# Hybrid decoder step: token numbers of the first expert pass from rank products on TensorE, router products on unscaled rows, and the samples' state product placed between the memory heads

## The chip, the core and the metric

The kernel runs on one core of one Trainium2 chip. The metric is the device time of one launch in microseconds (us), as the median of several runs. The core's engines run their own instruction streams side by side and wait for each other through semaphores: PE (TensorE, matrix products and transposes), DVE (VectorE), ACT (ScalarE), POOL (GpSimd, which here also issues the indirect DMAs), and SP (SyncE, which here only issues DMAs, so it is called the load queue).

## The reference, cut to what matters

One layer of a decoder trunk handles 512 prompt tokens and 8 sample tokens (520 rows of width 1024). A mixer with two head groups (a matrix memory of four heads, and windowed attention of eight heads) is followed by a mixture of 32 experts of which each token takes four:

```
z  = rms_norm(x, norm1) @ w_in                    # one projection for both groups
m  = matrix memory of 4 heads over z              # samples: from a given state C (8,4,64,128)
a  = window attention of 8 heads over z           # samples: over a cache of 128 keys
y  = x + concat(m, a) @ w_out
xn = rms_norm(y, norm2)
logits = xn @ w_router + b_router                 # (520, 32)
top 4 of 32, gates = softmax of the four
for every expert: rows that chose it -> w_gate, w_up, w_down (all 1024 x 1024), times gate
y  = y + sum over the four experts;  out = rms_norm(y, final_norm)
```

For the samples the memory's result needs q @ C, q.k and q.n for each of the 32 pairs of sample and head, and a new state C' = decay C + k v. Those are what "the samples' state product" and "the state update" mean below.

## The kernel before

The work runs in four stages, and each engine's order is the order in which its program is written.

1. **Projection, attention and memory heads** (to about 230 us of the span). The memory heads go in 12 turns (`UNIT_TURN`); a unit is a head h and a block of 128 keys, 16 units in all. In each turn DVE multiplies a unit's weights by PE's scores (`products_of_turn`, L1250), makes the next unit's weights (`weights_of_turn`, L1241), and after a head's last unit closes the head (`finish_head`, L1263 to L1283). The four turns before the last eight ride on projection steps; the last eight (4 to 11) each begin with a filler on PE, one part of the output projection over the attention half (`out_part`). PE's value products of head 3 wait until `finish_head(2)` has emptied PSUM (`num_used`).
2. **From the heads to the first output rows.** ACT and DVE normalise the heads' rows, PE transposes them, DVE multiplies them by the output gate (`mixm_made`, L1322, after the sigmoid, `og_ready`). The samples' gates take an exponential, a logarithm and three more exponentials on ACT (L903 to L909), with four small DVE operations between (L1310 to L1316). The samples' state, 1 MB, is loaded into the buffer that held the heads' rows, so the load (L525) waits for the heads' transposes; then DVE multiplies it by the samples' queries and adds up (L1344 to L1352, the result is `part`), and PE sums `part` across partitions (`dsum`). PE's order is: `project(0)`, the replication of gates and values (`rep`), `dsum`, a few small sample products (`own`), `project(1)`. `project(i)` finishes the output projection of 128 rows. POOL adds the residual (L649): the prompt rows of tile 0 are loaded again (L527) once the stores of the prompt's final state have landed.
3. **Routing.** For each of four tiles of 128 rows and one tile of 8 samples: DVE adds the halves (`add_up`), ACT takes squares and a square root (`squares`), DVE scales the row by it and by norm2 (`scale_rows`, L1374), PE transposes the scaled row and ACT copies it (`evac_x2`), PE makes the logits with `w_rt` (`route`), DVE finds the top four (`choose`, which also ends with the gates and the combined gate table g3), PE counts how many earlier rows chose each expert (`ranks`), and DVE turns expert and rank into a place in a table (`places`, L1381 to L1386). The sample tokens' attention is woven between the tiles, and `mixs_ready` (the samples' mixed rows) releases the samples' output projection, `project(4)`. When `project(4)` is over, the load queue may begin with the expert weights: 1 MB pieces, 12 for an expert, in a ring of 8.
4. **Experts.** POOL writes each chosen (token, gate) pair to its place in a table in DRAM: 20 indirect DMAs, four a tile (L663, first after `mixs_ready`). When all 20 have landed it reads the table back (L668), copies the token numbers out of it (`pass_tok`, L681), gathers the rows of the first two experts (L676), and stores the starting sums of the output to DRAM (`acc_rows`, L690), which has to have landed before an expert's output is added (`added`). Meanwhile PE, ACT and DVE make the experts' output biases for all rows (L1540) and split the first three weight pieces into a rounded part and a rest (L1026 on ACT, L438 on DVE). Then a loop runs over the 32 experts: 12 pieces each, every piece split by ACT and DVE and multiplied by PE with 12 products of 128 x 96 by 512 columns (L1618).

## Time and profile before

| | |
|---|---|
| median of 3 runs | 1583.27 us (1581.88 to 1585.08) |
| the profiled execution | 1581.5 us, span 1579.8 us |
| busy share of the span | PE 93%, DVE 80%, ACT 67%, POOL 12% |
| mean granted clock of PE | 0.952 of full speed |
| the expert loop on PE (L1618, 128 x 96 by 512) | 4608 products, 1100.0 us |
| DMA | 464.78 MB, mean 294 GB/s |

The span is what the profiler covers of one launch. Busy shares are averages over stages with different limits: three quarters of the span is the expert loop, and the change touches only what stands between the projections and the loop's start, about 200 to 410 us.

### The profile page before, as it was taken

The page shows a single profiled execution, that of the slowest core. Times are in us where ns is not written, and L with a number is a line of the kernel's source. Part 1 is how long each engine was busy: PE and PEld are TensorE (multiplying, and loading weights), DVE is VectorE, ACT ScalarE, POOL GpSimd, SP SyncE. Part 2 cuts the span into 40 slices and gives each one's busy share as a digit, 9 for nine tenths or more (in the row PEclk, how much of TensorE's full clock was granted, in tenths as well). Part 3 has the DMA queues.
Part 4 walks back from the last instruction along what each step waited for, and adds up shares of the span by engine and source line. Part 5 has one row for each costly group of instructions (what it writes and reads, how often), then busy time and mean ns, then how long its engine had stood idle before and what let it go on. Part 6 is the DMA issues. An engine that isn't in the chain of part 4 may idle for free.

```text
span 1579.8 us, 21342 instructions
## 1 busy us (share of the span) xinstructions
PE 1462.6 (93%) x7155; PEld 1069.2 (68%) x7155; DVE 1264.5 (80%) x1175; ACT 1057.3 (67%) x961; POOL 183.2 (12%) x183
## 2 busy tenths in 40 slices
PE   6999985774999999999999999999999999999993
PEld 5999764652676767676676767676766767676762
DVE  4344357335798999999999999999999998999995
ACT  4455333332678777777777777777777777777874
POOL 3000012026001110000000011000000001100000
PEclk9999996765899999999999999999999999999997
DMA  7311315016899999999999999999999999999994
GB/s 220 115 54 55 87 46 139 31 32 237 302 369 368 367 355 371 365 378 369 374 367 369 369 361 370 357 375 370 381 364 370 369 366 366 363 369 360 383 353 152
DMA packets 170588, 464.78 MB, mean 294 GB/s; under 512 B 14220, under 2 KB 28184, under 8 KB 170280
## 3 DMA queue, kind: packets, MB, share of 16 engines
q1 hardware_dynamic: 157528, 432.03, 74.2%
q0 software_dynamic: 8880, 24.00, 6.5%
q10 hardware_dynamic: 4144, 8.31, 1.6%
q8 instruction: 18, 0.29, 0.1%
q14 instruction: 18, 0.15, 0.0%
HBM read 447.90 MB, written 23.59 MB: 298 GB/s over the span
## 4 chain that ended last, share of the span: by engine, by line
PE 65%; issue 13%; DVE 11%; ACT 5%; DVEq 2%; DMA 1%; ACTq 1%; POOL 1%; POOLq 0%; SPq 0%
PE ps L1618 62%; DVE ring_r L438 6%; PE ps L1621 3%; ACT ring_r L1026 2%; DVEq L1587 1%; ACT reg_a L1039 1%; DVE reg_b L1581 1%; DVE reg_b L1576 1%; DMA acc_rows<-reg_z 0%; DMA reg_b<-in_state_C 0%; DMA acc_rows<-reg_a,pass_tok 0%; ACT L726 0%; POOLq L683 0%; ACT ring L1087 0%; ACT reg_z L934 0%
## 5 line engine op out<-in xcount | busy, mean ns | idle before, releaser
L1618 PE MATMUL ps<-ring_r,reg_z_r 128*96 128x512 f32 x4608 | 1100.0, 395 | 7.7 <-DVE reg_z_r L1546 7.6
L1618 PEld LDWEIGHTS ps<-ring_r,reg_z_r 128*96 128x96 f32 x4608 | 737.4, 162 | 322.6 <-DVE ring_r L438 11.0
L438 DVE TENSOR_TENSOR ring_r<-ring,ring_r 128x2048 fp32r<-128x2048 f32 x387 | 868.1, 2283 | 81.7 <-ACT ring_r L1026 81.7
L1026 ACT ACTIVATE ring_r<-ring 128x2048 fp32r<-128x2048 f32 x387 | 735.8, 1915 | 166.7 <-PE ps L1618 165.7
L705 POOL DMA_INDIRECT acc_rows<-reg_a,pass_tok x32 | 46.1, 1441 | 1030.6 <-issue 994.3
L1618 PE MATMUL ps<-reg_a_r,ring_r 128*128 128x264 f32 (+1 forms) x576 | 110.1, 286 | 0.0
L1045 ACT ACTIVATE reg_z_r<-ps 128x384 fp32r<-128x384 f32 x130 | 59.0, 480 | 66.9 <-PE ps L1621 66.9
L1618 PE MATMUL ps<-ring_r 128*128 128x256 f32 (+3 forms) x372 | 103.7, 328 | 0.0
L1618 PEld LDWEIGHTS ps<-reg_a_r,ring_r 128*128 128x128 f32 x576 | 90.6, 188 | 2.4 <-issue 2.2
L676 POOL DMA_INDIRECT reg_a<-xhat_rows,pass_tok x34 | 71.6, 2106 | 20.8 <-issue 20.8
L1618 PEld LDWEIGHTS ps<-ring_r 128*128 128x128 f32 (+1 forms) x372 | 67.5, 183 | 8.8 <-issue 3.5
L1546 DVE TENSOR_TENSOR reg_z_r<-ps,reg_z_r 128x384 fp32r<-128x384 f32 x130 | 65.7, 546 | 9.5 <-ACT reg_z_r L1045 9.5
L1039 ACT ACTIVATE reg_a<-ps,reg_t 96x512 f32<-96x512 f32 x66 | 41.6, 679 | 15.5 <-PE ps L1618 15.3
L1588 DVE SCALAR_TENSOR_TENSOR reg_x<-reg_x,reg_b 96x512 f32<-96x512 f32 x64 | 44.1, 689 | 4.8
L863 ACT ACTIVATE reg_z<-ps 128x256 f32<-128x256 f32 (+1 forms) x36 | 13.8, 384 | 45.6 <-PE ps L1618 45.6
L1064 ACT ACTIVATE reg_b<-reg_b 96x1024 f32<-96x1024 f32 x32 | 34.0, 1064 | 14.2 <-DVE reg_b L1576 14.0
L1586 DVE TENSOR_SCALAR reg_x<-ps 96x512 f32<-96x512 f32 x64 | 43.4, 678 | 0.0
L1621 PE MATMUL ps<-ident,reg_a 96*128 96x96 f32 x264 | 27.9, 249 | 15.0 <-DMA reg_a<-xhat_rows,pass_tok 15.0
L1186 DVE SCALAR_TENSOR_TENSOR reg_w<-ps,reg_b 128x512 f32<-128x512 f32 (+1 forms) x16 | 10.0, 625 | 39.4 <-PE ps L1618 39.4
L1576 DVE TENSOR_SCALAR reg_b<-ps 96x512 f32<-96x512 f32 x64 | 40.9, 678 | 0.0
L1621 PEld LDWEIGHTS ps<-ident,reg_a 96*128 96x128 f32 x264 | 26.1, 143 | 21.0 <-issue 15.9
L1130 DVE TENSOR_TENSOR ring_r<-ring,ring_r 128x2048 fp32r<-128x2048 f32 x13 | 29.8, 2289 | 13.1 <-ACT ring_r L759 13.1
(302 smaller groups left out, 942.6 us busy)
## 6 DMA issues: line engine op xcount, KB each, us to landing
ring<-in_w_gate SPq DMA_DIRECT2D x131, 1024.0 KB, 7.3
ring<-in_w_up SPq DMA_DIRECT2D x128, 1024.0 KB, 5.3
ring<-in_w_down SPq DMA_DIRECT2D x128, 1024.0 KB, 8.5
ring<-in_w_in SPq DMA_DIRECT2D x9, 1024.0 KB, 6.6
ring<-in_w_out SPq DMA_DIRECT2D x4, 1024.0 KB, 5.2
ring<-in_x_prompt SPq DMA_DIRECT2D x4, 512.0 KB, 8.6
reg_x<-in_x_prompt SPq DMA_DIRECT2D x4, 512.0 KB, 7.0
xhat_rows<-reg_w ACTq DMA_DIRECT2D x4, 512.0 KB, 3.7
```

Of the source, the lines that this page charges most:

```text
L438: return eng.tensor_tensor(rest_r(k), w, rounded_r(k).bitcast(F32), ALU.subtract)
L676: pool.indirect_dma_start(xg[0:CAP, u, :], None, xhat_rows[:, :], bass.IndirectOffsetOnAxis(pass_tok[0:CAP, e:e + 1], 0), bounds_check=TT ...
L705: pool.indirect_dma_start(acc_rows[:, :], bass.IndirectOffsetOnAxis(pass_tok[0:CAP, e:e + 1], 0), yrow[0:CAP, u, :], None, bounds_check=AC ...
L1026: act.activation(rounded_r(k), ring[:, slot_of(k), :], ACT.Copy).then_inc(hi_ready, 1)
L1039: last = act.activation(yrow[0:CAP, u, 512 * q:512 * q + 512], ps[4 + q][0:CAP, :], ACT.Copy, scale=slot_tab[:, bass.ds(t2 + 1, 1)])
L1045: last = act.activation(out[:, 0, 4 * q:4 * q + 4, :], ps[bank + q][:, 0:4 * CAP].rearrange("p (c n) -> p c n", c=4), ACT.Copy)
L1546: last = dve.tensor_tensor(out[:, 1, 4 * q:4 * q + 4, :], ps[bank + q][:, 0:4 * CAP].rearrange("p (c n) -> p c n", c=4), out[:, 0, 4 * q:4 ...
L1576: last = dve.tensor_scalar(eG[0:CAP, 512 * q:512 * q + 512], ps[q][0:CAP, :], LIMIT, None, ALU.min)
L1586: dve.tensor_scalar(hrow[0:CAP, cs], ps[2 + q][0:CAP, :], LIMIT, -LIMIT, ALU.min, ALU.max)
L1588: dve.scalar_tensor_tensor(hrow[0:CAP, cs], hrow[0:CAP, cs], 1.0, eS[0:CAP, cs], ALU.add, ALU.mult).then_inc(h_ready, 1)
L1618: return pe.matmul(out, lhsT, rhs, start=start, stop=stop, skip_group_check=True)
L1621: return pe.transpose(out, in_, ident[0:k, 0:k])
```

## The change

**The samples' state product.** The state gets a buffer of its own (`c_state` in the ring's scratch, `c_prod` and `c_half` in the buffer of the heads' rows), so its load no longer waits for the heads' transposes: it is issued with the other sample inputs. POOL makes the sample masks after unit 6 and not after unit 15. DVE multiplies and adds up one half of the state after turn 7 and the other after turn 8, and does the gates' small operations after turns 7 and 9; ACT does their exponentials and logarithm in turns 8 and 10. After the heads, ACT takes the sigmoid first; PE makes `rep` before the heads' transposes and `dsum` before `project(0)`. The state update moves from behind `add_up(0)` to ahead of it.

**The router on unscaled rows.** norm2 is multiplied into `w_rt` once; `route` transposes the rows of y1 and no longer those of xhat; the logits are multiplied by the row's factor in `choose`. `scale_rows` and the gates (`gates_of`) move behind `choose` and `places`.

**Token numbers from rank products.** For each tile `places` also makes, for each of the four choices, a one-hot of the rank over 96 places (`at_rank`) and the token number in the chosen expert's column (`at_expert`); PE multiplies them (`slots_of`, four products of 96 x 32), and DVE adds the tiles up into `pass_tok`. POOL gathers the first two experts' rows as soon as `pass_tok` is there, and then makes the last four table entries, reads the table back (it still holds the gates) and stores the starting sums.

```diff
-            dve.wait_ge(dec_in, 16 * (DEC_IN - 1))
-            dve.wait_ge(masks_made, 1)
-            dve.scalar_tensor_tensor(d32[:, 0:1], gpre[:, 1:2], -1.0, gpre[:, 1:2], ALU.mult, ALU.max).then_inc(sample_dve, 1)
+                if turn == 7:
+                    dve.wait_ge(dec_in, 16 * DEC_IN)
+                    dve.wait_ge(masks_made, 1)
+                    dve.scalar_tensor_tensor(d32[:, 0:1], gpre[:, 1:2], -1.0, gpre[:, 1:2], ALU.mult,
+                                             ALU.max).then_inc(sample_dve, 1)
+                    query_states(0, part_half)
+                if turn == 8:
+                    query_states(1, part[:, 0:DV])
...
-            dve.tensor_tensor(p_v, c_v, q16.unsqueeze(2).to_broadcast([P, 16, DV]), ALU.mult)
...
-            dve.tensor_reduce(part[:, 0:DV], c_prod.rearrange("p (k v) -> p v k", k=16), AX_X, ALU.add)
...
+            dve.wait_ge(late_in, 64)
+            dve.tensor_tensor(w_rt, w_rt, cols[:, 8:16].unsqueeze(2).to_broadcast([P, KC, NE]), ALU.mult)
...
+                dve.scalar_tensor_tensor(id4[0:r, :], rank4[0:r, :], -1.0, own_id[0:r, i:i + 1].to_broadcast([r, TOPK]),
+                                         ALU.mult, ALU.add)
+                dve.tensor_tensor(at_rank[0:r], iota_r[0:r].unsqueeze(1).to_broadcast([r, TOPK, CAP]),
+                                  rank4[0:r, :].unsqueeze(2).to_broadcast([r, TOPK, CAP]), ALU.is_equal)
+                dve.drain()
+                dve.tensor_tensor(at_expert[0:r], rt_oh[i % 2][0:r].rearrange("p e k -> p k e"),
+                                  id4[0:r, :].unsqueeze(2).to_broadcast([r, TOPK, NE]), ALU.mult).then_inc(sel_ready, 1)
...
-                pe.wait_ge(xhat_ready, i + 1)
+                pe.wait_ge(y_ready, 2 * i + 2)
...
-                        last = tr(ps[4 + q][:, c * P:c * P + r], xhat[0:r, i % 2, (4 * q + c) * P:(4 * q + c + 1) * P], r)
+                        last = tr(ps[4 + q][:, c * P:c * P + r], y1[0:r, i, (4 * q + c) * P:(4 * q + c + 1) * P], r)
...
+            def slots_of(i):
+                r = rows(i)
+                pe.wait_ge(sel_ready, ROUTE_ORDER.index(("p", i)) + 1)
+                for k in range(TOPK):
+                    last = mm(ps[7][0:CAP, P:P + NE], at_rank[0:r, k, :], at_expert[0:r, k, :],
+                              start=(k == 0), stop=(k == TOPK - 1))
+                last.then_inc(rank_psum, 1)
...
+            pool.wait_ge(count_ready, 1)
+            gather(0, 0)
+            gather(1, 1)
+            scatter_entries(NT)
```

On DVE, in turns 6 to 8 of the heads, before: the rest of a weight piece (L1130), products and weights of units 11 to 13.

```order
L1130 TENSOR_TENSOR ring_r_61<-ring,ring_r_61 128x2048
L1250 TENSOR_TENSOR reg_t<-reg_t,ps 128x256
L1241 TENSOR_SCALAR reg_t<-reg_w,small 128x128
L1130 TENSOR_TENSOR ring_r_61<-ring,ring_r_61 128x2048
L1250 TENSOR_TENSOR reg_t<-reg_t,ps 128x128
L1241 TENSOR_SCALAR reg_w<-reg_w,small 128x512
L1241 TENSOR_SCALAR reg_w<-reg_w,small 128x384
L1250 TENSOR_TENSOR reg_w<-reg_w,ps 128x512
L1250 TENSOR_TENSOR reg_w<-reg_w,ps 128x384
```

And after the change, over the same turns (`reg_b` is now the half product, `reg_w` and `reg_c` the sums of the halves):

```order
L1153 TENSOR_TENSOR ring_r_63<-ring,ring_r_63 128x2048
L1332 SCALAR_TENSOR_TENSOR ring<-ring 32x1
L1312 TENSOR_TENSOR reg_b<-ring 128x1024
L1315 TENSOR_REDUCE reg_w<-reg_b 128x128
L1273 TENSOR_TENSOR reg_t<-reg_t,ps 128x128
L1264 TENSOR_SCALAR reg_w<-reg_w,small 128x512
L1264 TENSOR_SCALAR reg_w<-reg_w,small 128x384
L1312 TENSOR_TENSOR reg_b<-ring 128x1024
L1315 TENSOR_REDUCE reg_c<-reg_b 128x128
L1337 TENSOR_TENSOR ring<-ring 128x16
L1339 TENSOR_TENSOR reg_c<-reg_c,reg_w 128x128
```

The two halves of the state (the 128x1024 products and the 128x128 sums) now stand among the units' products; the rows L1344 to L1352 of before, behind the heads, are gone.

On POOL, from the pads of the tables to the starting sums, before:

```order
L657 ISA
L663 DMA slot_rows<-reg_t,entry_at 21504x2 x20
L668 DMA reg_t<-slot_rows 96x7x64
L672 TENSOR_LOAD count_i
L672 ISA x2
L681 COPY pass_tok<-reg_t 96x34
L676 DMA reg_a<-xhat_rows,pass_tok 96x1024 x2
L690 DMA acc_rows<-reg_z 128x1024 x4
L690 DMA acc_rows<-reg_z 8x1024
L691 DMA acc_rows<-reg_z 96x1024
```

And after:

```order
L672 ISA
L677 DMA slot_rows<-reg_t,entry_at 21504x2 x16
L689 DMA reg_a<-xhat_rows,pass_tok 96x1024 x2
L677 DMA slot_rows<-reg_t,entry_at 21504x2 x4
L704 DMA reg_t<-slot_rows 96x7x64
L706 TENSOR_LOAD count_i
L706 ISA x2
L709 DMA acc_rows<-reg_z 128x1024 x4
L709 DMA acc_rows<-reg_z 8x1024
L710 DMA acc_rows<-reg_z 96x1024
```

The two gathers have moved from behind the read-back of the table to ahead of the last four entries, and the starting sums follow the read-back.

On PE, from the heads' transposes to `project(1)`, before:

```order
L1621 MATMUL ps<-ident,reg_b 128x128 x16
L1618 MATMUL ps<-ring_r_61,reg_a_r_62 128x512 x24
L1618 MATMUL ps<-ring 128x130
L1618 MATMUL ps<-reg_t,ring 32x130
L1618 MATMUL ps<-ring 64x130
L1618 MATMUL ps<-ring 64x128
L1621 MATMUL ps<-ident,ring 128x64
L1618 MATMUL ps<-ring_r_61,reg_a_r_62 128x512 x24
```

And after:

```order
L1684 MATMUL ps<-ring 128x130
L1687 MATMUL ps<-ident,reg_b 128x128 x16
L1684 MATMUL ps<-reg_c,ring 32x130
L1684 MATMUL ps<-ring_r_63,reg_a_r_64 128x512 x24
L1684 MATMUL ps<-ring 64x130
L1684 MATMUL ps<-ring 64x128
L1687 MATMUL ps<-ident,ring 128x64
L1684 MATMUL ps<-ring_r_63,reg_a_r_64 128x512 x24
```

`rep` (128x130) and `dsum` (32x130) have moved ahead of `project(0)` (the first 24 products).

## Rows read from the trace of the kernel before

**Rows 1.** Busy by stretch: length, PE, PEld, DVE, ACT, POOL, clock, DMA, GB/s

```profile
230.00:262.00 32.00, 13.81 (x46) 10.43 (x47) 23.19 (x37) 12.22 (x17) 11.12 (x14) 0.65 0.60 157
262.00:357.00 95.00, 71.18 (x293) 54.57 (x291) 40.68 (x132) 31.38 (x52) 12.57 (x11) 0.69 0.14 44
357.00:397.00 40.00, 14.60 (x67) 10.34 (x67) 19.58 (x39) 11.72 (x16) 23.57 (x23) 0.52 0.71 255
```

**Rows 2.** Waits of the load queue, 500 to 1500: total, times, longest

```profile
SPq L113 <- PE ps L1618: 788.5, 334, 3.5
```

**Rows 3.** Chain that ended last: start, us, what; heads to project(1)

```profile
237.40 1.28 ACT L903
...
244.13 6.30 DMA reg_b<-in_state_C
250.45 2.29 DVE ring L1344
...
255.11 3.65 DVE reg_t L1347
...
263.08 7.43 PE ps L1618 x24
```

**Rows 4.** Waits by engine, 240 to 480: total, times, longest

```profile
PE ps L1618 <- ACT reg_z L934: 11.8, 5, 4.1
...
PE ps L1621 <- DVE reg_w L1374: 7.5, 2, 5.0
...
PE ps L1618 <- DVE entry_at L1386: 2.5, 1, 2.5
```

**Rows 5.** Timeline of PE: start, us, what, count, idle before

```profile
222.84 1.83 PE L1618 MATMUL ps<-reg_t,reg_w 128*128 128x129 f32 x14
...
246.98 8.58 PE L1618 MATMUL ps<-ring_r,reg_a_r 128*128 128x512 f32 x24 [2.89 <-issue]
...
356.66 0.16 PE L1621 MATMUL ps<-ident 1*1 1x1 f32 x1
...
397.10 1.17 PE L1618 MATMUL ps<-reg_t_r,reg_p_r 128*96 128x512 f32 x2 [2.08 <-DVE reg_z_r L1546]
```

**Rows 6.** Timeline of DVE, same columns

```profile
219.73 0.76 DVE L1273 TENSOR_TENSOR reg_b<-ps,gsc 128x256 f32<-128x256 f32 x2
...
252.66 2.38 DVE L1345 TENSOR_TENSOR ring<-ring 128x16 f32<-128x16 f32 x1
...
373.57 6.27 DVE L1540 TENSOR_TENSOR reg_z<-reg_z,ps 128x512 f32<-128x512 f32 x10 [2.63 <-PE ps L1618]
...
379.89 6.68 DVE L438 TENSOR_TENSOR ring_r<-ring,ring_r 128x2048 fp32r<-128x2048 f32 x3
```

**Rows 7.** Timeline of POOL, same columns

```profile
251.83 5.50 POOL L649 TENSOR_TENSOR reg_z<-reg_z,reg_x 128x1024 f32<-128x1024 f32 x2 [19.27 <-DMA reg_x<-in_x_prompt]
...
345.79 1.12 POOL L663 DMA_INDIRECT slot_rows<-reg_t,entry_at  x1 [1.02 <-issue]
...
368.10 0.98 POOL L663 DMA_INDIRECT slot_rows<-reg_t,entry_at  x1 [0.30 <-issue]
```

**Rows 8.** Timeline of the load queue: the reload of prompt tile 0

```profile
244.75 0.33 SPq L527 DMA_DIRECT2D reg_x<-in_x_prompt  x1
```

**Rows 9.** Chain that ended last, from project(4) to the expert loop

```profile
364.22 0.18 DVE reg_t L1392
...
366.04 2.35 PE ps L1618 x10
...
374.71 4.46 issue
...
382.38 4.26 POOLq L683
...
389.29 1.04 POOL reg_a L676
...
394.34 7.66 DMA acc_rows<-reg_z
```

More of the change, by code:

```diff
@@ L253, in hybrid_step @@
         q16, k16, n16, kw16 = d_in[:, 0:16], d_in[:, 16:32], d_in[:, 32:48], d_in[:, 48:64]
-        part = reg_t[:, 0:132]
+        part = reg_c[:, 2048:2048 + 132]
+        part_half = reg_w[:, 1540:1540 + DV]
         part2 = part[:, 0:130]
@@ L657, in _, with scatter_entries @@
             pool.engine_nop().then_inc(pads_made, 1)
-            pool.wait_ge(tab_init, 16)
-            for i in range(NTILE):
+            def scatter_entries(i):
                 pool.wait_ge(entries_ready, i + 1)
@@ L666, in _ @@
                         bounds_check=PASSES * CAP * NE - 1, oob_is_err=False).then_inc(entries_out, 16)
-            pool.wait_ge(entries_out, ENTRIES)
-            pool.dma_start(slot_tab[:, 2:2 + (PASSES + 1) * TABW].rearrange("p (a n) -> p a n", a=PASSES + 1), slot_pages).then_inc(tab_in, 16)
+            pool.wait_ge(tab_init, 16)
+            for i in range(NT):
+                scatter_entries(i)
             pool.wait_ge(xhat_out[0], 16 * 3)
             pool.wait_ge(xhat_out[1], 16 * 2)
-            pool.wait_ge(count_ready, 1)
-            most = pool.value_load(count_i[0:1, 0:1], min_val=0, max_val=TT)
-            pool.wait_ge(tab_in, 16)
             def gather(u, e):
@@ L1285, in finish_head, with query_states @@
                     last.then_inc(hss_ready, 1)
+            def query_states(half, out):
+                c_v = c_state[:, D * half:D * half + D].rearrange("p (k v) -> p k v", k=8)
+                dve.tensor_tensor(c_half.rearrange("p (k v) -> p k v", k=8), c_v,
+                                  q16[:, 8 * half:8 * half + 8].unsqueeze(2).to_broadcast([P, 8, DV]), ALU.mult)
+                dve.drain()
+                dve.tensor_reduce(out, c_half.rearrange("p (k v) -> p v k", k=8), AX_X, ALU.add)
+                dve.drain()
             dve.wait_ge(zs_out, 16 * 10)
@@ L1404, in choose, with gates_of @@
                 dve.tensor_reduce(chosen[0:r, i, :], rt_oh[i % 2][0:r], AX_X, ALU.add).then_inc(sel_ready, 1)
+            def gates_of(i):
+                r = rows(i)
                 dve.wait_ge(gexp_ready, i + 1)
@@ L1408, in choose @@
                 dve.tensor_scalar(gate4[0:r, :], gexp[0:r, :], rs1[0:r, 2:3], None, ALU.mult)
-                dve.tensor_scalar(entry[0:r, i, :, 1], gexp[0:r, :], rs1[0:r, 2:3], None, ALU.mult)
+                last = dve.tensor_scalar(entry[0:r, i, :, 1], gexp[0:r, :], rs1[0:r, 2:3], None, ALU.mult)
+                if i == NT:
+                    last.then_inc(entries_ready, 1)
                 dve.drain()
@@ L1458, in _ @@
             dve.tensor_reduce(d32[:, 10:11], s32, AX_X, ALU.add).then_inc(sample_dve, 1)
-            scale_rows(1)
             dve.wait_ge(drms_ready, 1)
@@ L1476, in _ @@
             dve.tensor_copy(o64, ps[3][0:64, 0:P]).then_inc(own_used, 1)
+            dve.wait_ge(iotas_made, 1)
+            norm_of(0)
             choose(0)
+            gates_of(0)
+            scale_rows(0)
             add_up(2)
@@ L1484, in _ @@
             dve.tensor_scalar(ds[:, 1:2], ds[:, 0:1], ds[:, 5:6], -1.0, ALU.max, ALU.mult).then_inc(sample_dve, 1)
-            scale_rows(2)
+            norm_of(1)
             choose(1)
             places(0)
+            gates_of(1)
+            scale_rows(1)
             add_up(3)
@@ L1500, in _ @@
             dve.tensor_scalar(a64, a64, ds[:, 6:7], None, ALU.mult).then_inc(sample_dve, 1)
-            scale_rows(3)
+            norm_of(2)
             choose(2)
             places(1)
+            gates_of(2)
+            scale_rows(2)
+            norm_of(3)
             choose(3)
             places(2)
+            gates_of(3)
+            scale_rows(3)
             dve.wait_ge(mixs_psum, 1)
@@ L1901, in _ @@
             mm(ps[2][0:32, 256:386], g4, part2).then_inc(sample_pe, 1)
+            project(0)
             pe.wait_ge(*q2_ready)
@@ L1947, in _ @@
             ranks(4)
+            slots_of(4)
             for j in range(NTILE):
```

223 lines of the change are left out of this document (124 added, 99 removed).

## The prediction

> **What bounds the kernel now.** I read first the waits inside the expert loop, then the busy time by stretch, and then the chain of waits through the stretches where no engine is full.
>
> In the loop the load queue waits for PE to give a ring slot back: 334 times, 788.5 us in all [rows 2]. Weights are asked for as fast as PE lets go of them, so PE is the limit there, and a loop that begins x us earlier ends x us earlier. The change touches nothing inside it. The heads before 230 us are full on PE too. The room is between: PE is busy for 13.8 of 32 us, 71.2 of 95 and 14.6 of 40, at a granted clock of 0.65, 0.69 and 0.52 [rows 1]. Three things make PE wait there.
>
> 1. *Heads to project(1).* The 1 MB state load takes 6.30 us, the product over the state 2.29, its sum 3.65; from the load's issue at 244.13 to project(1) at 263.08 the chain holds nothing else of size [rows 3]. project(0), at 246.98, lies beside the load [rows 5].
> 2. *Routing.* PE waits 11.8 us over five tiles for ACT's copies of the transposed rows, 7.5 for scaled rows and 2.5 for table places [rows 4].
> 3. *project(4) to the loop.* project(4) ends at 356.66 and the loop's first product is at 397.10 [rows 5]. The chain is a table in DRAM: the last entry's landing (4.46 us from 374.71), the read-back, a 4.26 us copy on POOL, the gathers at 389.29, the starting sums landing from 394.34 to 402.0 [rows 9].
>
> **The change, step by step.** The sum is made as microseconds off the start of the loop.
>
> *State product among the heads.* Half the state should take half of 2.29 and 3.65 us [rows 3] and a little start-up, so about 1.2 + 1.85; twice that, and some 2 us of small operations, make 8 us more for DVE in turns 7 to 9. DVE has that time, but the close of head 2 moves back. Today its last multiply ends at 220.5 and PE wants it at 222.84 [rows 5, 6], a slack of 2.3 us. By my schedule of DVE's order the close is some 2.8 us later, so PE waits 0.5. If the sum over a half cost as much as the whole one does now, DVE would be 3.6 us later and PE would wait about 4. I take a loss of 0.5, bounds 0 and 4. The state's load now lands some 13 us before turn 7 ends, so nothing waits for it.
>
> *Heads to project(1).* Off ACT's path between the heads and the output gate go three table loads of 1.28 us like the one at 237.40 [rows 3] and DVE's four small operations; the sigmoid is over before the heads' square root is. The gate's multiplies start about 4.3 us earlier, so project(0) starts near 242.7 instead of 246.98 and, at its 8.58 us [rows 5], ends near 251.3; the small products `own` take it to 252.5. project(1) then needs tile 0 added up, which needs two things. DVE does the state update first: the router scaling, 2.29 for the outer product and as much again for the decay, done near 250.3. And POOL's residual add: the prompt tile is asked for at 244.75 [rows 8], when the stores of the final state have landed, which the change leaves alone. Today it has landed by 251.83, with 1 MB of state beside it; now it is alone. I expect 4 us, so the add (half of 5.50 [rows 7]) runs from about 249 to 252, and tile 0 is added up near 253. project(1) starts at 253.5: 9.5 us gained. Bounds: 7.5 if the tile lands no sooner than today, 10.5 if it is never late.
>
> *Routing.* The waits of PE that go: nearly all of the 11.8 us for copies (ACT no longer stands in DMA issues, table loads and keys while the transposed rows wait), the 2.5 for a scaled row that isn't the last tile's (7.5 less 5.0), and 2.5 for places: 16.8 us. What comes back: a copy's own time before each router product, about 0.65 for four tiles, 2.6; the products of `slots_of`, at most 0.9 a tile if each costs as much as the products in `ranks` (2.35 us for ten halves [rows 9]), 2.7 for three tiles; PE's wait for `places(2)`, which now also makes the one-hots (a 128 x 384 compare near 0.6, two small ones 0.45), about 3; the samples' keys, whose copy now stands behind a square and a square root that wait for a store, 2; and the samples' mixed rows, behind one more `scale_rows`, 1.7. That is 12, so 4.5 us gained; bounds 1 and 9.
>
> *project(4) to the loop, on POOL.* Choosing for tile 4 starts today at 364.22 [rows 9], 7.6 us after project(4). Of the 5.0 us that PE now waits for that tile's scaled row [rows 4] some 2.3 go, since its transposes begin right behind the sums, while the copies stand behind ACT's square and square root: choosing starts at 5.3. Choosing and ranking (to 368.4 today) take 4.2 as now, `places` with its one-hots 2.1, `slots_of` and the last addition 1.2: token numbers at 12.8. The sixteen entries of tiles 0 to 3 stand ahead of the gathers on POOL; they took 345.79 to 369.1 [rows 7], that is, to 12.4 after project(4), and hang on the samples' mixed rows as project(4) does. So both come together. Then two gathers at 1.04 and four entries at 0.98, each with 0.30 between [rows 7, 9], 2.7 and 5.1; the entries' landing 4.46; the read-back's issue and the count's read 1.5, an estimate; the stores, as today from the gathers' end near 391.7 to 394.34, 2.7; their landing 7.66 [rows 9]: 36.9. Today 402.0 is 45.3 after project(4). Gain 8.4.
>
> *The same stretch on DVE and PE.* From 12.8: tile 4's gates 1.8, transposes of the gate table and their copy 2.1, the biases 1.3 and 6.27 [rows 6], the pick 0.3, the three rests 6.68 [rows 6], the rest of the gathered rows 1.0, hand-overs 0.8: the loop's first product 32.8 after project(4), against 40.4. Gain 7.6. The gathers land behind the biases, where they have 6 us; the read-back and POOL's copy, now of two columns, lie beside the stores. ACT splits the fourth piece only after the starting sums, so the two chains tie. I take 7.5; bounds 4 and 9.
>
> Sum: 9.5 - 0.5 + 4.5 + 7.5 = 21.0. The profiled execution took 1581.5 us (span 1579.8 and 1.7 around it) and would come to 1560.5; it lies 1.8 under the median of the runs, 1583.27, so I forecast 1562.
>
> **A lock that speaks against it.** At 252.66 a product of 16 elements took 2.38 us on DVE while POOL ran its residual adds from 251.83 [rows 6, 7]: an operation with two operands in SBUF stood still for one of POOL's. By that row the new state update, which runs into the same adds, may be held by one (2.75) and hold one in turn, and the sum would be 18.3. The Trainium skill, "SBUF — State Buffer", section "SBUF: two separate sides", says that VectorE and GpSimd share a port pair under an exclusive lock held for the whole instruction; the trace agrees with the 2.38 us. By my times the update is over as the adds begin, so I keep 21.
>
> **The rivals.**
> - *The lock or POOL's queue eats part of it.* Either the update and the adds meet (18.3 above), or POOL is later than DVE: each 0.1 us more for an entry puts the gathers 1.6 later, and the gathers now pass through the same queue ahead of the last entries while weights stream in, so that the landing of 4.46 may grow to 8 or 9. Then the starting sums come 4 us later and the loop with them: 17. If both, 13. For it: both are seen in today's rows. If the gathers had to wait as long as for the table, the token numbers would have done nothing, and the third term would be near 2: 15.5.
> - *The weight stream decides.* If the loop went at the pace of its loads, only project(4)'s end would count: 13.5. Against it: 334 waits for PE [rows 2].
> - *More than that.* With fewer waits PE's clock, 0.65 to 0.69 in the two stretches [rows 1], rises: the 71 us that PE is busy from 262 to 357 shrink by some 5: 26.
> - *Slower.* DVE's new work in turns 7 to 9 makes PE wait for head 2. PE's clock fell to 0.65 where it stood idle after the heads [rows 1]; a wait of several us would run the last 7 us of the heads at the lower level (1.2 instead of 2.4 GHz), 7 more. The wait itself would have to pass 14 us to eat all of 21: DVE would need over 16 us beyond its slack, where I count 2.8 us. That is 1585.
> - *Nothing gained*, because some wait I don't see releases the loop at the old time.
>
> **How the numbers follow.** Forecast (gain of 18 to 24) 0.52; lock or POOL's queue (11 to 18) 0.22; weight stream (13.5) 0.06; more (24 to 30) 0.15; nothing 0.03; slower 0.02. The predicted time is that of the first, 1562, with 1559 to 1565 as its own range. A range from 1556 to 1572 takes in the second and third cases and most of the fourth. A change under 0.2% (3.2 us) can't be told from none here; by the cases, faster by more than that 0.95, within it 0.03, slower 0.02.
>
> **What would show it.** After: project(1) near 254, project(4) ending near 343, the loop's first product near 376 and the starting sums landed near 380; PE's waits for copies under 1 us each; `finish_head(2)` ending near 223; no wait of the gathers' transposes for DMA. It is wrong if PE stands in the heads after 222 for over 2 us, if the residual add ends after 254, if the gathers' rows land after 370, or if waits for loads appear in the loop.

## The result, and the profile after

The changed kernel took 1558.33 us (median of 4 runs, 1556.17 to 1560.30) against 1583.76 (4 runs, 1581.88 to 1585.08): a ratio of 0.984, 95% interval 0.9821 to 0.9859. The profiled execution took 1559.85 us, its span is 1558.1, against 1581.5 and 1579.8: 21.7 us less between the two traces. 1562 was forecast, with 1556 to 1572 as its range.

| mark, us from the span's start | before | forecast | after |
|---|---|---|---|
| project(0) begins | 246.98 | 242.7 | 245.01 |
| project(1) begins | 263.08 | 253.5 | 254.55 |
| project(4) ends | 356.66 | 343 | 340.61 |
| loop's first product | 397.10 | 376 | 374.07 |
| starting sums landed, POOL goes on | 402.0 | 380 | 380.4 |

Busy time by stretch after the change, in the columns of [rows 1]: the same three stretches, and then the one from project(1)'s begin to project(4)'s end.

```profile
230.00:262.00 32.00, 22.03 (x90) 16.69 (x89) 20.89 (x43) 9.54 (x13) 7.89 (x16) 0.79 0.67 171
262.00:357.00 95.00, 66.00 (x329) 51.99 (x330) 46.94 (x162) 33.44 (x57) 25.79 (x22) 0.71 0.26 92
357.00:397.00 40.00, 29.39 (x103) 18.49 (x103) 26.13 (x26) 21.75 (x18) 9.89 (x14) 0.72 0.83 278
254.55:340.77 86.22, 64.31 (x300) 49.36 (x300) 42.12 (x141) 30.33 (x51) 16.79 (x13) 0.74 0.20 51
```

The first three rows hold more of PE's work than before, at a higher clock. They are the same clock times but no longer the same work, so the fourth row is the one to compare by: 86.2 us, of which PE is busy 64.3 and idle 21.9. In the trace of before project(1) to project(4)'s end takes 93.7, busy 70.1 and idle 23.6, at 0.69:

```profile
263.08:356.82 93.74, 70.10 (x289) 53.94 (x288) 39.52 (x131) 30.60 (x52) 11.49 (x11) 0.69 0.14 45
```

The timeline of PE after the change (start, us, what, count, idle before), answering [rows 5]:

```profile
225.45 1.80 PE L1684 MATMUL ps<-reg_t,reg_w 128*128 128x129 f32 x14 [0.71 <-DVE reg_b L1296]
...
245.01 8.10 PE L1684 MATMUL ps<-ring_r,reg_a_r 128*128 128x512 f32 x24 [2.15 <-issue]
...
254.55 5.83 PE L1684 MATMUL ps<-ring_r,reg_a_r 128*128 128x512 f32 x24 [0.66 <-DVE reg_z L1410]
267.45 1.08 PE L1687 MATMUL ps<-ident,reg_c 128*128 128x128 f32 x4 [7.07 <-DVE ring L1510]
...
285.02 3.56 PE L1684 MATMUL ps<-ring,reg_b 128*128 128x8 f32 x16 [6.00 <-ACT reg_b L988]
...
340.61 0.16 PE L1687 MATMUL ps<-ident 1*1 1x1 f32 x1
...
374.07 1.17 PE L1684 MATMUL ps<-reg_t_r,reg_p_r 128*96 128x512 f32 x2 [6.12 <-DVE reg_z_r L1612]
...
387.35 3.01 PE L1684 MATMUL ps<-ring_r,reg_z_r 128*96 128x512 f32 x12 [1.68 <-DVE ring_r L449]
```

Two waits stand out in the routing. PE waits 7.07 us ahead of the samples' keys' transposes for the end of a gate chain on DVE (L1494 to L1510), and 6.00 us ahead of their products for ACT's copy of the keys. In the trace of before the same two waits were 3.44 and 3.74:

```profile
273.94 1.09 PE L1621 MATMUL ps<-ident,reg_c 128*128 128x128 f32 x4 [3.44 <-DVE ring L1458]
...
295.30 3.55 PE L1618 MATMUL ps<-ring 128*128 128x8 f32 x16 [3.74 <-ACT ring L964]
```

DVE and POOL around the first of them, and DVE's new halves of the state product:

```profile
217.51 1.22 DVE L1312 TENSOR_TENSOR reg_b<-ring 128x1024 f32<-128x1024 f32 x1
218.80 1.91 DVE L1315 TENSOR_REDUCE reg_c<-reg_b 128x128 f32<-128x1024 f32 x1
...
261.78 0.34 DVE L1499 SCALAR_TENSOR_TENSOR ring<-ps,ring 32x128 f32<-32x128 f32 x1
262.05 1.68 DVE L1500 SCALAR_TENSOR_TENSOR ring<-ring 32x1 f32<-32x1 f32 x1
263.80 2.22 DVE L1502 TENSOR_TENSOR ring<-ring 32x1 f32<-32x1 f32 x1
```

```profile
251.17 4.96 POOL L664 TENSOR_TENSOR reg_z<-reg_z,reg_x 128x1024 f32<-128x1024 f32 x2 [15.89 <-DMA reg_x<-in_x_prompt]
261.36 4.65 POOL L664 TENSOR_TENSOR reg_z<-reg_z,reg_x 128x1024 f32<-128x1024 f32 x2 [5.23 <-DMA reg_x<-in_x_prompt]
355.87 1.00 POOL L689 DMA_INDIRECT reg_a<-xhat_rows,pass_tok  x1 [2.13 <-DVE pass_tok L1592]
...
368.28 0.89 POOL L704 DMA_DIRECT2D reg_t<-slot_rows  x1 [5.41 <-DMA slot_rows<-reg_t,entry_at]
```

Two operations on 32 elements take 1.68 and 2.22 us while POOL's residual adds of tiles 2 and 3 run, from 261.36 to 266.01. POOL's last two rows show the gathers right behind the token numbers, and the read-back of the table only after a 5.41 us landing of the last entries. ACT at the loop's entry:

```profile
371.64 0.87 ACT L1068 ACTIVATE reg_z_r<-ps 128x384 fp32r<-128x384 f32 x2 [7.47 <-DMA reg_t<-slot_rows]
380.62 1.28 ACT L1062 ACT_TABLE_LOAD   x1 [8.10 <-POOLq L716]
```

It rounds the first gathered rows only when the read-back has landed, though PE had transposed them by 367.95, and goes on only when POOL lets it.

### The profile page after: what moved, and what is told of

The parts are those of the page before. It is cut to its first block, busy times and chain, and to the rows that moved or that the text cites. A ratio compares the mean times of both kernels' runs of the same rounds, so it can differ in the third digit from the quotient of the medians.

```text
span 1558.1 us, 21411 instructions
## 1 busy us (share of the span) xinstructions
PE 1458.3 (94%) x7175; PEld 1065.6 (68%) x7175; DVE 1269.5 (81%) x1199; ACT 1054.3 (68%) x959; POOL 179.7 (12%) x186
## 4 chain that ended last, share of the span: by engine, by line
PE 61%; issue 18%; DVE 10%; ACT 5%; DVEq 2%; DMA 2%; POOL 1%; ACTq 1%; SPq 0%; POOLq 0%
PE ps L1684 58%; DVE ring_r L449 6%; PE ps L1687 3%; ACT ring_r L1049 2%; DVEq L1653 2%; ACT reg_a L1062 1%; DVE reg_b L1647 1%; DVE reg_b L1642 1%; DMA reg_x<-in_x_prompt 1%; DMA out_p_n<-reg_x 1%; POOL reg_z L664 0%; DMA acc_rows<-reg_a,pass_tok 0%; ACT ring L1110 0%; ACT L1062 0%; POOL slot_rows L677 0%
## 5 line engine op out<-in xcount | busy, mean ns | idle before, releaser
L1684 PEld LDWEIGHTS ps<-ring_r,reg_z_r 128*96 128x96 f32 x4608 | 737.5, 162 | 323.9 <-DVE ring_r L449 12.5
L1062 ACT ACTIVATE reg_a<-ps,reg_t 96x512 f32<-96x512 f32 x66 | 41.5, 679 | 15.5 <-PE ps L1684 15.3
L1153 DVE TENSOR_TENSOR ring_r<-ring,ring_r 128x2048 fp32r<-128x2048 f32 x13 | 29.8, 2289 | 13.1 <-ACT ring_r L782 13.1
L1647 DVE TENSOR_TENSOR reg_b<-reg_b 96x1024 f32<-96x1024 f32 x32 | 38.9, 1215 | 0.0
```

What stands on the lines that cost most here:

```text
L1062: last = act.activation(yrow[0:CAP, u, 512 * q:512 * q + 512], ps[4 + q][0:CAP, :], ACT.Copy, scale=slot_tab[:, bass.ds(t2 + 1, 1)])
L1647: dve.tensor_tensor(eS[0:CAP, :], eS[0:CAP, :], eG[0:CAP, :], ALU.mult)
L1684: return pe.matmul(out, lhsT, rhs, start=start, stop=stop, skip_group_check=True)
```

## The experiments

Each kernel is the changed kernel with one edit, loop_entry, loop_entry_2 and the last two with several together. Those timed together shared a chip and its runs of the kernel before; every ratio is to the kernel before. The last column is the ratio less 0.984, times 1584 us.

| kernel | median us | ratio (95%) | against the changed kernel, us |
|---|---|---|---|
| undo_state | 1567.90 | 0.9894 (0.9877 to 0.9911) | +8.6 |
| undo_router | 1571.44 | 0.9923 (0.9909 to 0.9937) | +13.1 |
| undo_tokens | 1563.41 | 0.9868 (0.9853 to 0.9883) | +4.4 |
| table_gather | 1567.64 | 0.9899 (0.9884 to 0.9914) | +9.3 |
| adds_late | 1555.72 | 0.9823 (0.9809 to 0.9836) | -2.7 |
| route_first | 1554.85 | 0.9812 (0.9799 to 0.9826) | -4.4 |
| keys_first | 1555.70 | 0.9820 (0.9807 to 0.9834) | -3.2 |
| stores_first | 1559.66 | 0.9843 (0.9829 to 0.9856) | +0.5 |
| loop_entry | 1559.38 | 0.9852 (0.9839 to 0.9866) | +1.9 |
| loop_entry_2 | 1550.29 | 0.9801 (0.9788 to 0.9815) | -6.2 |
| all_parts | 1544.42 | 0.9761 (0.9748 to 0.9775) | -12.5 |
| all_parts_2 | 1535.54 | 0.9705 (0.9692 to 0.9719) | -21.4 |

The changed kernel's ratio is known to 3.0 us and most of the others to 2.1, so a difference under some 3.7 us can't be told by the times alone. adds_late, keys_first, stores_first and loop_entry are under it, and undo_tokens and route_first hardly over. adds_late, route_first, keys_first and stores_first ran on one chip; no run of the first three (1552.5 to 1558.8) is over the median of the fourth, 1559.7. That speaks for a gain of the three, if stores_first stands for the changed kernel there.

### Each part undone

**undo_state.** The state product, its load and the small operations go back behind the heads:

```diff
-                if turn == 7:
-                    query_states(0, part_half)
...
+            dve.wait_ge(dec_in, 16 * DEC_IN)
+            query_states(0, part_half)
+            query_states(1, part[:, 0:DV])
...
+            sp.wait_ge(hT_psum, MH)
             sp.dma_start(c_state, ...)
```

> The changed kernel with the samples' state product and its load put back behind the memory heads (router and token numbers as changed). By the prediction's terms the 9.5 us before project(1) come back and the 0.5 in the heads goes: 9.0 slower than the changed kernel's 1558.3, so 1567.3, with project(1) again some 8 to 9 us later. Rival, that the residual add of tile 0 (behind the store of the final state, 8.8 us) now sets project(1) whatever the product does: under 4 us lost, 1562 or less.

Measured: 1567.90, +8.6. PE around it:

```profile
248.49 8.18 PE L1684 MATMUL ps<-ring_r,reg_a_r 128*128 128x512 f32 x24 [2.88 <-issue]
...
262.42 0.64 PE L1684 MATMUL ps<-reg_c,ring 128*32 128x130 f32 x2 [5.33 <-DVE reg_c L1384]
...
264.33 7.20 PE L1684 MATMUL ps<-ring_r,reg_a_r 128*128 128x512 f32 x24
```

project(1) begins at 264.33, 9.8 us later, and what PE waits for is the state's sum. The first term is confirmed, the rival (under 4 us) is not.

**undo_router.** Scaled rows are transposed, the router's weights are unscaled, and ACT's and DVE's order is that of before:

```diff
-                pe.wait_ge(y_ready, 2 * i + 2)
+                pe.wait_ge(xhat_ready, i + 1)
...
-                        last = tr(ps[4 + q][:, c * P:c * P + r], y1[0:r, i, ...], r)
+                        last = tr(ps[4 + q][:, c * P:c * P + r], xhat[0:r, i % 2, ...], r)
```

> The changed kernel with the router's products on scaled rows again, in the order of before (state product and token numbers as changed). By the prediction's routing sum this part alone is worth 16.8 of waits less 2.6 (copies), 2 (keys) and 1.7 (mixed rows), 10.5, and 2.3 more of tile 4's scaled row behind project(4): 12.8 slower, 1571. Rival, that project(4) hangs on the samples' attention chain and not on the router's waits: 5 slower or less, 1563.

Measured: 1571.44, +13.1. The waits come back as they were in [rows 4], here by engine with total, times and longest, 225 to 400:

```profile
PE ps L1684 <- ACT reg_z L958: 11.6, 4, 4.9
PE ps L1687 <- DVE reg_w L1420: 8.2, 2, 5.8
```

That 13.1 is so near 12.8 is partly chance. Between project(1) and project(4) PE's idle time is 28.4 us against 21.9, 6.5 more where 10.5 was expected. The other 5.1 us of this stretch are busy time (69.4 against 64.3), which differs as much between runs of one program, as the section on PE's clock shows.

**undo_tokens and table_gather.** The first takes out the one-hots and their products and lets the gathers wait for the table. The second keeps the one-hot work and only lets the gathers wait:

```diff
-            pool.wait_ge(count_ready, 1)
-            gather(0, 0)
-            gather(1, 1)
-            scatter_entries(NT)
             pool.wait_ge(entries_out, ENTRIES)
...
+            pool.wait_ge(tab_in, 16)
+            slots_of_pass(0)
+            gather(0, 0)
+            gather(1, 1)
```

> The changed kernel without the one-hot work, the gathers waiting for the table again (state product and router as changed). By the prediction's terms the table costs some 4.6 us behind project(4) (40.4 less the 2.3 that the router part gives, against the 33.5 now), and the routing is 5.7 quicker without the one-hots and their products: within 2 us of the changed kernel, 1557. Rival, that the one-hot work lies in waits that PE has anyway: 4 to 6 slower, 1563.

> The changed kernel with all the one-hot work kept, but the gathers waiting for the table again. The third term by itself: the table chain behind project(4) against the token numbers, 5 to 7 us slower, 1564. The difference to the kernel without the one-hot work is that work's price in the routing: 5.7 by the prediction, near 0 by the rival. If the stall at the loop's entry is set by the starting sums alone, under 2 us slower, 1560.

Measured: 1563.41 (+4.4) and 1567.64 (+9.3). Both are dearer than the prediction's terms gave (2 at most, and 5 to 7); the first came out at its rival's 4 to 6. One reason is what POOL and PE show; first undo_tokens, then table_gather:

```profile
363.32 0.21 POOL L695 COPY pass_tok<-reg_t 96x34 uint32<-96x34 uint32 x1 [2.36 <-DMA reg_t<-slot_rows]
366.17 7.02 POOL L690 DMA_INDIRECT reg_a<-xhat_rows,pass_tok  x1 [2.63 <-issue]
```

```profile
369.59 4.32 POOL L694 COPY pass_tok<-reg_t 96x34 uint32<-96x34 uint32 x1 [2.38 <-DMA reg_t<-slot_rows]
...
380.79 1.51 PE L1683 MATMUL ps<-ident,reg_a 96*128 96x96 f32 x8 [14.99 <-DMA reg_a<-xhat_rows,pass_tok]
```

DVE splits three weight pieces without a pause from 365.60 to 372.3 in the one and from 367.16 to 373.8 in the other. The one kernel has its copy of 0.21 us ahead of them and its first gather's issue, 1.0 elsewhere, takes 7.02; the other has its copy among them, at 4.32. The copy and the gather's issue end about where the splits end. Not all that POOL does there waits: in the changed kernel five issues of plain stores at 369.58 take 2.74 us beside the splits (366.41 to 373.1), as long as in the trace of before, where no split runs beside them. The token numbers bring the gathers ahead of the splits. How much of the 9.3 us that is worth, and how much is the table's own chain, was not tried apart.

What the one-hots cost in the routing these runs leave open between 2 and 5.5 us. In the stretch from project(1) to project(4) the two differ by 2.2 (86.3 us against 84.1). The expectation had named the difference of the times, which is 4.2; of it 2.3 lie ahead of project(1) in the two profiles (255.10 against 252.82), where PE's clock from 20 to 40 us was 0.91 and 0.99. And in five profiles with the same program in that stretch, its length goes from 86.2 to 89.6 (below).

### Where the time is still lost

**adds_late.** POOL's residual adds of tiles 2 and 3 wait for the gate chain:

```diff
+                if i == 2:
+                    pool.wait_ge(*dss_ready)
```

> The changed kernel, with one wait more on POOL: its residual adds of tiles 2 and 3 begin only when the samples' gate chain on DVE is done. If POOL's adds hold DVE (two operations of 32 elements took 1.68 and 2.22 us inside the adds), these two take about 0.15 each, PE's wait before the keys' transposes falls from 7.07 to about 3.5, and the time by 3.5, to 1554.8. Rival, that the two operations are late for another reason, or that the wait is no longer on the path: the same, 1558.3. If the moved adds then hold other operations of DVE, the gain is under 1.5.

Measured: 1555.72, -2.7. DVE's two operations, and PE behind them:

```profile
262.77 0.14 DVE L1502 SCALAR_TENSOR_TENSOR ring<-ring 32x1 f32<-32x1 f32 x1
262.98 0.15 DVE L1504 TENSOR_TENSOR ring<-ring 32x1 f32<-32x1 f32 x1
```

```profile
264.55 0.85 PE L1689 MATMUL ps<-ident,reg_c 128*128 128x128 f32 x4 [3.43 <-DVE ring L1512]
```

1.68 and 2.22 became 0.14 and 0.15, and PE's wait 3.43: it was POOL's adds that held them. That much is shown; the gain in time is within its interval. The other side of this is in the windows below.

**route_first.** PE does tile 0's router before the keys' transposes:

```diff
+            route(0)
             pe.wait_ge(cache_in, 32)
             pe.wait_ge(*dss_ready)
             keys_T(0)
-            route(0)
```

> The changed kernel, with tile 0's transposes and router products ahead of the keys' transposes in PE's order, so that they lie in the 7.07 us that PE waits for the samples' gate chain. If that wait is on the path that sets the end, about 4.2 us (the transposes, the wait for their copy and the products, less what the chain is still late) come off: 1554. Rival, that the routing's pace is set by the samples' attention chain or by POOL's entries and not by PE there: the same, 1558.

Measured: 1554.85, -4.4. The transposes, the wait for their copy and the products went into the wait, 3.45 us of it stayed (7.07 before). DVE was held again, at another operation:

```profile
259.31 2.31 DVE L1496 TENSOR_SCALAR ring<-ring 32x128 f32<-32x128 f32 x1
261.55 0.26 DVE L1497 TENSOR_SCALAR ring<-ps,ring 32x1 f32<-32x1 f32 x1
```

**keys_first.** ACT copies the keys before it waits for tile 0's scaled row:

```diff
+            round_keys(0)
+            round_keys(1)
             store_xhat(0)
...
-            round_keys(0)
             squares(2)
-            round_keys(1)
```

> The changed kernel, with ACT's two copies of the samples' keys ahead of the store of tile 0's scaled row and the bias loads. The prediction took 2 us for the keys behind a square that waits; the trace shows PE waiting 6.00. If the store's wait for DVE's scaled row is what holds the keys, PE's wait falls to about 1 and the time by 4 to 5: 1553.8. Rival, that PE then waits as long for the next thing of the attention chain: the same, 1558.

Measured: 1555.70, -3.2. The wait for the keys is nearly gone, but the next one on the same engine has grown, from 0.69 to 3.14 us, since the second tile's copies now stand behind a square that waits:

```profile
284.12 1.92 PE L1685 MATMUL ps<-ring,reg_b 128*128 128x8 f32 x16 [0.78 <-ACT reg_b L984]
...
290.12 3.62 PE L1685 MATMUL ps<-reg_p,reg_z 128*128 128x32 f32 x16 [3.14 <-ACT reg_z L957]
```

**stores_first.** POOL issues the starting sums before the read-back:

```diff
             scatter_entries(NT)
-            pool.wait_ge(entries_out, ENTRIES)
-            pool.dma_start(slot_tab[...], slot_pages)
...
             pool.dma_start(acc_rows[TT:ACC_ROWS, :], y1[0:CAP, 0, :])
+            pool.wait_ge(entries_out, ENTRIES)
+            pool.dma_start(slot_tab[...], slot_pages)
```

> The changed kernel, with POOL issuing the stores of the starting sums ahead of its wait for the last entries and the table's read-back. The prediction had the two chains at the loop's entry tie (POOL 36.9 behind project(4), DVE and PE 32.8 with the fourth piece split only after the starting sums). The stores can go from about 363 as each tile's bias is added, the last at 367, landed near 375 against 380.6. By the tie, PE's stalls of 1.7 and 0.9 in the first turn go, 2.6 less at most: 1555.7. If POOL's chain is not on the path: 1558.3. If the read-back lands late among the stores (ACT's rounding of the gathered rows waits for it) it is slower, by up to 3.

Measured: 1559.66, no change that can be told. From issue to landing the read-back took 9.6 us behind the stores, against 3.3, so ACT rounded the gathered rows at 376.25 and PE's first product came at 378.23, later than in the changed kernel. In exchange PE had no stall before the fourth piece. What one wait lost (4.2 us at the first product), the other gave back in part (the 2.6 of stalls).

**loop_entry.** ACT rounds the gathered rows before it waits for the read-back, DVE takes their rest behind the first piece, and POOL signals before its wait for the stores' landing:

```diff
-            act.wait_ge(tab_in, 16)
             act.wait_ge(ex_psum, 1)
             round_blocks(eX, 6, 0, 2).then_inc(xhi_ready, 1)
+            act.wait_ge(tab_in, 16)
...
-            pool.wait_ge(acc_init, 16 * (NTILE + 1))
             pool.engine_nop().then_inc(added, 3)
+            pool.wait_ge(acc_init, 16 * (NTILE + 1))
```

> The changed kernel with the loop's entry reordered: POOL lets ACT go on without waiting for the landing of the starting sums (POOL itself still waits for it ahead of its first scatter-add), ACT rounds the first gathered rows before it waits for the table's read-back, and DVE takes their rest behind the first of the three pieces. If these two waits (ACT 3.7 us for the read-back, 8.1 for the starting sums) are what holds the first turn, the first product goes from 374.1 to about 370.1 and the stalls of 1.7 and 0.8 behind it go: 6.4 less, 1552. If only the first product counts and the stalls stay: 4 less, 1554. If the weights' landing decides there, as the late starting sums of the run before suggest: the same, 1558.

Measured: 1559.38, +1.9: the time of the third expectation, but not for its reason. PE's first product came at 369.07, sooner than the first one wanted, and then PE waited 5.40 for the fourth piece. The chain of waits says why:

```profile
371.50 1.96 POOL pass_tok L712
373.46 5.91 issue
379.37 0.02 POOLq L715
```

POOL's signal is L715. It came no sooner than before, though nothing but a drain stands between it and the copy at L712. That the drain lasts until the stores, issued just ahead, have landed is my reading; it was not tried by itself.

**loop_entry_2.** The signal is moved ahead of the read-back and the stores:

```diff
             scatter_entries(NT)
+            pool.engine_nop().then_inc(added, 3)
             pool.wait_ge(entries_out, ENTRIES)
```

> The reordered entry again, but POOL lets ACT go on ahead of the read-back and the stores. In the run before, the first product came 5 us earlier and PE then waited 5.4 for the fourth piece, because POOL, having issued the stores at 371.4, reached its signal to ACT only at 379.4. If that signal is all that holds the fourth piece, the 5.4 go and the time falls by 5 to 6.5 against the changed kernel: 1552 to 1553. Rival, that the loads of the weights set the fourth piece or one behind it: under 2 less, 1557.

Measured: 1550.29, -6.2, and the stall is gone: four pieces (48 products) run without a gap.

```profile
370.17 1.17 PE L1685 MATMUL ps<-reg_t_r,reg_p_r 128*96 128x512 f32 x2 [2.02 <-DVE reg_z_r L1612]
371.14 13.04 PE L1685 MATMUL ps<-ring_r,reg_z_r 128*96 128x512 f32 x48
```

So the two waits of ACT were both on the path, and the loads were not.

**all_parts and all_parts_2.** adds_late, route_first and keys_first together, in the last with ACT's second tile's copies ahead of the square; the first with loop_entry, the second with loop_entry_2.

> The changed kernel with the late adds, tile 0's router ahead of the keys' transposes, the keys' copies first (and now also the second tile's copies ahead of the square that waits), and the reordered entry. If the four waits are separate, their gains add: 2.6 and 3.5, 2.6 to 5 for the keys, and what the entry gives (4 to 6.4): 13 to 17 less, 1541 to 1545. If they cover each other (the samples' attention chain sets the routing's end whatever PE does), 8 less or under, 1550.

> All parts, with the entry of the run beside it. The run before of all parts had 8.1 us of wait before the fourth piece; without it 1536. Rival, that the loads set the pieces there, now that the loop is asked for 15 us earlier: 1542 or more, with waits for loads in ACT's splits of the first pieces.

Measured: 1544.42 and 1535.54. The second is 0.9705 of the kernel before and the best of this study. The four alone sum to 16.5 (2.7, 4.4, 3.2 and 6.2), and together, with the keys' part made whole, they gave 21.4: they don't cover each other, and nothing in the samples' attention chain kept the routing from becoming 13 us shorter.

### PE's clock in the routing

One row of windows for each kernel, from project(1)'s begin to project(4)'s end, in the columns of [rows 1]: undo_state, undo_router, undo_tokens, adds_late, keys_first, all_parts_2 (its row begins 0.2 us ahead of project(1)).

```profile
264.33:351.94 87.61, 72.00 (x301) 56.47 (x300) 43.02 (x144) 31.62 (x52) 10.85 (x11) 0.67 0.14 48
```

```profile
255.40:353.20 97.80, 69.44 (x300) 54.70 (x300) 42.59 (x141) 30.12 (x51) 16.77 (x13) 0.70 0.15 43
```

```profile
252.82:336.91 84.09, 64.84 (x288) 49.94 (x288) 37.78 (x126) 30.28 (x51) 16.31 (x13) 0.72 0.19 51
```

```profile
255.26:339.03 83.77, 67.21 (x300) 52.31 (x300) 38.66 (x141) 30.38 (x51) 16.29 (x13) 0.71 0.20 52
```

```profile
254.49:339.81 85.32, 68.57 (x300) 52.21 (x300) 40.40 (x142) 29.92 (x51) 17.15 (x13) 0.69 0.18 50
```

```profile
252.20:325.10 72.90, 63.14 (x300) 48.23 (x300) 42.05 (x143) 30.22 (x51) 17.20 (x13) 0.74 0.23 61
```

And three kernels whose edits lie behind project(4), so that their program in this stretch is the changed kernel's: stores_first, loop_entry, loop_entry_2.

```profile
254.45:340.64 86.19, 64.50 (x300) 49.23 (x300) 42.37 (x142) 30.25 (x51) 17.13 (x13) 0.72 0.19 51
```

```profile
252.66:340.18 87.52, 67.51 (x300) 52.55 (x300) 41.59 (x141) 30.34 (x51) 16.32 (x13) 0.71 0.19 50
```

```profile
252.62:342.17 89.55, 70.47 (x300) 54.32 (x300) 42.64 (x142) 30.38 (x51) 17.35 (x13) 0.68 0.18 49
```

The same 300 matrix instructions (288 in undo_tokens) keep PE busy from 63.1 to 72.0 us, by and large the longer the lower the granted clock. adds_late took 5.3 us of idle time out of this stretch (16.6 against 21.9), and 2.9 came back in busy time; keys_first took out 5.2 and 4.3 came back. But what came back can't be put down to these edits. With table_gather there are five profiles of the changed kernel's own program in this stretch: PE is busy for 64.3, 64.4, 64.5, 67.5 and 70.5 us in them, and idle for 21.9, 21.9, 21.7, 20.0 and 19.1. The changed kernel's profile is at the short end.

In part the two trade. In the changed kernel project(2) took 5.84 us and PE then waited 6.00 for ACT's copy of the keys; in loop_entry project(2) took 7.57 and the wait was 4.04. Another engine ends that wait, so slower products ahead of it cost next to nothing.

## Why the prediction was right, and where it was off

The time was inside the range and 3.7 us under the forecast. It was below the 1559 to 1565 of the first case: the gain of 25.4 us between the medians belongs to the case "more than that" (24 to 30), which had a chance of 0.15. Between the two traces it is 21.7 against the sum of 21.0, and that this is so near is luck. Four terms were off and cancel, and PE's clock differs between the two traces already ahead of the change.

- **Heads, 0.5 lost.** The halves took 1.22 and 1.91 us where 1.2 and 1.85 were taken, head 2's last multiply ended at 225.30 and PE waited 0.71. Right. That 225.30 is over the 223 that was named goes with the run. In it PE's granted clock was 0.88 from 20 to 40 us, in the input projections, against 1.00 in the run of route_first, which has the same heads. There the multiply ended at 223.30 and project(0) began at 243.01, 2.0 us sooner. In the trace of before that clock was 0.98.

```profile
20.00:40.00 20.00, 18.71 (x135) 15.21 (x134) 8.75 (x18) 6.37 (x14) 4.81 (x21) 0.88 0.43 138
```

```profile
20.00:40.00 20.00, 18.72 (x154) 16.32 (x152) 10.12 (x20) 6.51 (x14) 4.94 (x21) 1.00 0.44 140
```

- **Heads to project(1), 9.5.** 8.5 in the traces, with that late start in it; undone, this part with the heads costs 8.6 where 9.0 was expected. Right, with the step named for it: the residual add of tile 0 ended at 253.8 and DVE's addition began as it ended. The state update ended at 251.53, 0.36 us into that add, so the two met but hardly. In route_first project(0) begins at 243.01, the add at 249.43 and project(1) at 252.61, where 242.7, 249 and 253.5 had been named.
- **Routing, 4.5** (16.8 less 12 is 4.8). 7.5 in the traces, but not by the steps given. By these PE's idle time was to fall by 7.5: 16.8 us of waits go and 9.3 come back, since the 2.7 for `slots_of` are busy time. It fell by 1.7 only. The waits for places (3.13), for the mixed rows (1.8) and for the keys (6.00, 2.3 more than before) came as forecast. Those for copies fell from 11.5 in this stretch to 4.0, where 2.6 were to be left; the sign "under 1 us each" was missed by 1.48, 1.09 and, behind project(4), 2.31. And the wait for the gate chain, which stood in no term, rose from 3.44 to 7.07. The step that failed stands in "A lock that speaks against it": the lock was looked for at the state update, where the two hardly meet, and not ten microseconds later, where POOL's adds of tiles 2 and 3 fall on the samples' gate chain. That cost 3.6 (7.07 instead of 3.43, by adds_late), most of the 5.8 that are missing. The term for the one-hots, 5.7, is at the upper end of what the runs leave open (2 to 5.5) or above it: undo_tokens, without them, waits 1.9 for places and 3.0 instead of 1.8 for the mixed rows, so the 3 us for `places(2)` in part replace waits that PE has anyway. PE's busy time hid the miss. It fell by 5.8, though 2.4 us of `slots_of` were new in it. The rival "more than that" had priced such a fall at 5. How much of it the change brings is open: loop_entry_2, with the same routing, was busy for 70.5 us against the 70.1 of before, and its stretch was shorter by 4.2 only.
- **project(4) to the loop, 7.5.** 5.6 in the traces (21.7 less the 16.1 that project(4)'s end had gained). The first product came 33.5 us behind project(4), forecast 32.8 (its terms sum to 33.05); the starting sums 39.8, forecast 36.9. So the tie was no tie: POOL's chain set the fourth piece. The step that failed is "choosing starts at 5.3": it started 6.9 behind project(4), at 347.55, so the token numbers came at 14.3 instead of 12.8. The scaled row's multiply stood ahead of it on DVE until 5.85. For the last 1.09 the view names no engine of this core, and what it was stays open; in table_gather and loop_entry_2 DVE waited 0.47 and 0.48 there, for PE.

```profile
345.19 1.27 DVE L1420 SCALAR_TENSOR_TENSOR reg_w<-reg_z,small 8x1024 f32<-8x1024 f32 x1
347.55 0.24 DVE L1451 SCALAR_TENSOR_TENSOR reg_t<-ps,small,reg_t 8x32 f32<-8x32 f32 x1 [1.09 <-remote]
```

  The entries' landing took 5.41 instead of 4.46. ACT's wait for the read-back was in no term; in the changed kernel DVE's splits hide it, and loop_entry_2 shows that with both of ACT's waits gone 6.2 us more were to be had.
- **The rivals.** The weight stream decided nothing: loop_entry_2 and all_parts_2 began the loop's products 3.9 and 19.7 us earlier, and their spans are shorter by 8.5 and 24.6. "If both, 13" is 14.3 by its own terms (18.3 less 4). Gathers that wait as long as for the table would have come to 15.5; with the table they cost 9.3, and POOL waited only for the token numbers. The lock was real and elsewhere.

The three parts undone one at a time cost 8.6, 13.1 and 4.4: 26.1, and the whole change gave 25.4. Within their intervals they add.

The Trainium skill, "SBUF — State Buffer", section "SBUF: two separate sides", says that the lock on the shared ports goes to whichever starts first of a GpSimd operation and a DVE operation that is in a two-port mode or, against a GpSimd operation that reads SBUF, has two SBUF inputs. The 1.68 and 2.22 us beside POOL's adds and the 4.32 us copy beside DVE's splits agree with that. The same section says that a DMA issued from GpSimd can't write its descriptors while DVE runs in a two-port mode, and that `tensor_tensor`, which the splits are, was not seen to stall a DMA. The plain stores' 2.74 us agree with that; the 7.02 us of the gather's issue, in one profile, does not.

## What to carry to other kernels

When work is moved earlier, everything behind it moves too, and two engines that never met before may meet: list what each engine that shares a port with another will now do at the same time, over the whole stage and not only at the place of the edit. An engine that runs in order and also issues DMAs or signals others is late with all of them when it is late with one; here the same signal moved a few instructions, ahead of the DMA issues and their drain instead of behind them, made the difference between no gain and 6.2 us. Idle time taken from PE is not yet time: look at its granted clock and busy time in the same stretch before counting the wait as gained, and in more than one profile, since one program was busy there for 64.3 to 70.5 us.

## What the runs showed of the hardware

- DVE operations that read PSUM ran at 0.26 and 0.34 us within POOL's adds (L1497, L1499), those with all operands in SBUF stood until about where an add ended (1.68 from 262.05 and 2.22 from 263.80, with two adds in 4.65 us from 261.36; in route_first 2.31). One that had begun 0.12 us ahead of POOL's first add, at 261.24, took its usual 0.28.
- Beside DVE's splits of 128x2048, POOL's copy of 96x34 took 4.32 us (0.21 ahead of them in undo_tokens) and an indirect gather's issue 7.02 (1.00 elsewhere). Five issues of plain stores took their usual 2.74.
- One program kept PE busy for 64.3 to 70.5 us over the same 300 instructions, at a mean granted clock of 0.74 to 0.68, in five profiles.
- Between runs of one kernel the time goes with the clock of the whole run: the changed kernel's four took 1556.2 at 0.962, 1556.8 at 0.963, 1559.9 at 0.960 and 1560.3 at 0.957.
- POOL reached an instruction behind a drain 5.9 us after its last copy, with six DMA issues of up to 0.6 us just ahead of that copy.
